# One merged order for six expert jobs: the 192-token job's weight pieces placed between the chunks of the five 64-token jobs

## The reference

```python
def moe_swiglu(h, w_router, w_gate, w_up, w_down):
    xt = h.reshape(-1, d)                       # 264 x 1024
    top_v, top_i = lax.top_k((xt @ w_router), 2)
    wts = jax.nn.softmax(top_v, axis=-1)
    comb = jnp.einsum('tk,tke->te', wts, one_hot(top_i, 8))
    for e in range(8):
        he = silu(xt @ w_gate[e]) * (xt @ w_up[e])      # 1024 -> 3584
        y = y + comb[:, e:e + 1] * (he @ w_down[e])     # 3584 -> 1024
```

## Time and profile before

| | |
|---|---|
| median of 3 runs | 1712.05 us (1707.0 to 1712.27) |
| profiled execution, its own time | 1708.26 us |
| span of its instructions | 1706.4 us |
| TensorE busy | 1490.1 us, 87% |
| VectorE, ScalarE, GpSimd busy | 771.7, 633.9, 141.8 us |
| moved by DMA | 511.54 MB, mean 300 GB/s |
| mean granted clock of TensorE | 0.954 |

### The profile page before, as it was taken

One profiled execution on the slowest core, in us unless ns is written; L12 is line 12 of the kernel. 1 busy time (PEld: TensorE's weight loads), 2 busy tenths in 40 slices (PEclk: granted clock), 3 DMA queues, 4 the chain that ended last, 5 costly groups with the idle time before them and its releaser, 6 DMA issues.

```text
span 1706.4 us, 23857 instructions
## 1 busy us (share of the span) xinstructions
PE 1490.1 (87%) x9451; PEld 1069.2 (63%) x9451; DVE 771.7 (45%) x1096; ACT 633.9 (37%) x965; POOL 141.8 (8%) x209
## 2 busy tenths in 40 slices
PE   6989889999797897999999999998777878778771
PEld 3878779988585795888888666653333433334331
DVE  2554464566466945899998555520000101001013
ACT  3632354512346555788887454520000000000002
POOL 1032100000012201850000000000000000000001
PEclk9998899999987699999999999999999999999996
DMA  9751565345553266999997656579999999999995
GB/s 359 289 229 68 204 253 196 124 161 204 203 196 141 84 244 274 420 422 402 418 391 280 234 207 237 220 263 422 421 422 421 422 422 422 422 422 422 423 422 205
DMA packets 67432, 511.54 MB, mean 300 GB/s; under 512 B 7600, under 2 KB 7871, under 8 KB 15248
## 3 DMA queue, kind: packets, MB, share of 16 engines
q1 hardware_dynamic: 63730, 496.60, 73.1%
q0 software_dynamic: 3072, 12.54, 2.0%
q10 hardware_dynamic: 542, 1.20, 0.2%
HBM read 486.44 MB, written 23.89 MB: 299 GB/s over the span
## 4 chain that ended last, share of the span: by engine, by line
PE 35%; DMA 27%; DVE 2%; issue 1%; ACT 1%; SPq 0%; POOL 0%; DVEq 0%; ACTq 0%; POOLq 0%
PE bank L2119 34%; DMA ring<-in_expert_rows_dram 26%; DMA y_rows<-arena 1%; PE bank L2647 1%; DMA fT<-y_rows,row_i 0%; DVE arena L2100 0%; PE bank L2572 0%; DVE hT L1936 0%; DVE arena L2092 0%; ACT arena L1356 0%; DVE arena L2102 0%; SPq L607 0%; POOL arena L963 0%; DVE rstd L1505 0%; ACT plain_lo L1246 0%
## 5 line engine op out<-in xcount | busy, mean ns | idle before, releaser
L2119 PE MATMUL bank<-ring,fT 128*64 128x256 f32 (+1 forms) x2928 | 415.6, 424 | 93.1 <-DMA ring<-in_expert_rows_dram 90.1
L2119 PEld LDWEIGHTS bank<-ring,fT 128*64 128x64 f32 x2928 | 198.3, 136 | 293.7 <-DMA ring<-in_expert_rows_dram 127.7
L2119 PE MATMUL bank<-parts,w_hi 128*128 128x264 f32 x1600 | 309.9, 295 | 20.2 <-DVE parts L1512 20.1
L2119 PE MATMUL bank<-w_hi,parts 128*128 128x512 f32 x1008 | 303.4, 396 | 4.3 <-issue 2.6
L548 DVE TENSOR_TENSOR w_lo<-ring,w_hi 128x1024 fp32r<-128x1024 f32 x216 | 261.4, 1227 | 61.8 <-ACT w_hi L543 48.5
L2119 PEld LDWEIGHTS bank<-parts,w_hi 128*128 128x128 f32 x1600 | 259.0, 197 | 31.2 <-issue 18.9
L543 ACT ACTIVATE w_hi<-ring 128x1024 fp32r<-128x1024 f32 x216 | 228.5, 1062 | 116.4 <-PE bank L2119 115.4
L2119 PE MATMUL bank<-parts,w_lo 128*128 128x264 f32 x800 | 232.9, 291 | 0.0
L2119 PEld LDWEIGHTS bank<-w_hi,parts 128*128 128x128 f32 x1008 | 185.3, 188 | 58.1 <-issue 19.7
L2119 PE MATMUL bank<-w_lo,parts 128*128 128x512 f32 x504 | 182.9, 390 | 0.0
L497 DVE TENSOR_TENSOR w_lo<-ring,w_hi 128x2048 fp32r<-128x2048 f32 x50 | 114.3, 2291 | 141.0 <-ACT w_hi L491 140.9
(11 more groups left out here) (465 smaller groups left out, 1359.0 us busy)
## 6 DMA issues: line engine op xcount, KB each, us to landing
ring<-in_expert_rows_dram SPq DMA_DIRECT2D x294, 1024.0 KB, 15.2
ring<-in_dense_rows_dram SPq DMA_DIRECT2D x48, 2048.0 KB, 8.2
hT<-in_expert_rows_dram SPq DMA_DIRECT2D x49, 1024.0 KB, 15.1
ring<-in_dense_rows_dram SPq DMA_DIRECT2D x8, 1408.0 KB, 5.9
x_rows<-arena SPq DMA_DIRECT2D x1, 8192.0 KB, 30.5
y_rows<-arena SPq DMA_DIRECT2D x9, 512.0 KB, 13.4
arena<-x_rows SPq DMA_DIRECT2D x8, 512.0 KB, 15.9
y_rows<-arena SPq DMA_DIRECT2D x1, 3584.0 KB, 38.6
```

Of the source, the lines that this page charges most:

```text
L2119: return pe.matmul(out, lhsT, rhs, start=start, stop=stop, skip_group_check=True)
```

## The change

The jobs 2 to 7 become one unrolled order, `MIX`. It walks through the 35 chunks of the five 64-token jobs and places the 21 pieces of the 192-token job between them, one after about two of three chunks in the first 32. A piece of the 192-token job now does its four units of 128-token products first and then the raw products of all four units; a half is given back by the latter. In the mixed order the pieces of the 192-token job are not split ahead of the previous job's end; ScalarE and VectorE split a piece's four units at its place in the order. Each 64-token chunk has gate and up in one bank (`lot_bank`), and its SiLU comes when both are complete. The x rows of the 64-token jobs are packed (`LOT_ROW`, 64 rows each), fetched once during job 0 into `x_lots`, and turned from there. Results of 64-token jobs are stored as 64 rows by two DMAs (`store_lot`). `x_rows` and `y_rows` get smaller, and so do their zero fills (12 and 5 blocks of 128 rows, in place of 16 and 7). The prefetch after the last job is now inside the branch for overflow jobs. All loops over jobs are unrolled, GpSimd's table takes three more operations, and the semaphores of the first state and the router weights are merged.

```diff
-BIG_BLOCK = JOBS + 2
+BIG_OVER = 32
+LOT_ROW = P * (BIG + 2)
+OVER_ROW = LOT_ROW + LOT * HALF_JOBS
+BIG_ROW = OVER_ROW + P * OVER
+ROW_COUNT = BIG_ROW + LOT
...
+BIG_PIECES = [(f"big_{_w}", _c) for _c in range(NCHK) for _w in ("gate", "up", "down")]
+MIX, _placed = [], 0
+for _n in range(HALF_JOBS * NCHK):
+    _k, _c = divmod(_n, NCHK)
+    MIX.append(("gate", _k, _c))
+    if _c:
+        MIX.append(("turn", _k, _c - 1))
+    if _placed and BIG_PIECES[_placed - 1][0] == "big_up" and MIX[-2 - bool(_c)][0] == "big_up":
+        MIX.append(("big_turn", None, BIG_PIECES[_placed - 1][1]))
+    MIX.append(("up", _k, _c))
+    if _c:
+        MIX.append(("down", _k, _c - 1))
+    if _c == NCHK - 1:
+        if _k + 1 < HALF_JOBS:
+            MIX.append(("x", _k + 1, 0))
+        MIX += [("turn", _k, _c), ("down", _k, _c)]
+    while _placed < min(len(BIG_PIECES), len(BIG_PIECES) * _n // BIG_OVER):
+        _w, _b = BIG_PIECES[_placed]
+        MIX.append((_w, None, _b))
+        _placed += 1
...
+        x_lots = [arena[LOT * (k % 2):LOT * (k % 2) + LOT, D * (k // 2):D * (k // 2) + D] for k in range(HALF_JOBS)]
...
-            with eng.Fori(0, FULL_JOBS - 1) as j:
-                job(j, j, "full", "full")
-            job(FULL_JOBS - 1, FULL_JOBS - 1, "full", "big")
-            job(BIG, BIG, "big", "half")
-            with eng.Fori(0, HALF_JOBS) as k:
-                half_job(k + BIG + 1)
...
+        def lot_bank(c):
+
+            return bank[2 if c % 2 == 0 else 6]
+
+        def big_slot_free(eng, n):
+
+
+            if n < AHEAD:
+                unit_free(eng, BIG - 1, NU + n - AHEAD)
+                return
+            p, q = divmod(n - AHEAD, 4)
+            if q < 3:
+                eng.wait_ge(early_units_used, 3 * (EXPERT_PIECES * BIG + p) + q + 1)
+            else:
+                name, c = BIG_PIECES[p]
+                eng.wait_ge({"big_gate": gate_full, "big_up": up_full, "big_down": down_done}[name], NCHK * BIG + c + 1)
+
+        def for_jobs(eng, job, mix, first_units):
+
+
+            for j in range(FULL_JOBS):
+                job(j, j, "mix" if j == FULL_JOBS - 1 else "full")
             eng.wait_ge(jobs_ready, 2)
             more = eng.value_load(tabi[0:1, 0:1], min_val=0, max_val=OVER)
+            mix()
             with eng.If(more > 0):
-                if first_units:
-                    first_units(EXPERTS, BIG + 1)
                 with eng.Fori(0, more) as k:
-                    job(k + EXPERTS, k + BIG + 1, "full", "full")
-            return more + EXPERTS
-
-        def turn_banks(kind):
-
-            return (0, 2) if kind == "big" else (7, 2)
+                    first_units(k + EXPERTS, k + BIG + 1)
+                    job(k + EXPERTS, k + BIG + 1, "alone")
...
+                    zeros = y_job.rearrange("q a b -> q (a b)").unsqueeze(1).broadcast_to([P, ROW_COUNT // P, D])
                     sp.dma_start(x_rows.rearrange("(j p) d -> p j d", p=P), zeros).then_inc(x_zeroed, 16)
-                    sp.dma_start(y_rows[P * (EXPERTS + 1):P * (JOBS + 3), :].rearrange("(j p) d -> p j d", p=P),
-                                 zeros[:, 0:OVER + 2, :]).then_inc(x_zeroed, 16)
+                    sp.dma_start(y_rows[OVER_ROW:BIG_ROW, :].rearrange("(j p) d -> p j d", p=P),
+                                 zeros[:, 0:OVER, :]).then_inc(x_zeroed, 16)
...
-            rest(0, 0)
-            sp.dma_start(x_raw_b, x_rows[P * BIG_BLOCK:P * BIG_BLOCK + LOT, :]).then_inc(x_raw_loaded, 16)
+            rest_with_rows(0, 0)
+            sp.dma_start(x_raw_b, x_rows[BIG_ROW:BIG_ROW + LOT, :]).then_inc(x_lots_loaded, 16)
+            for at in range(0, LOT * HALF_JOBS, P):
+                n = min(P, LOT * HALF_JOBS - at)
+                sp.dma_start(arena[0:n, D * (at // P):D * (at // P) + D], x_rows[LOT_ROW + at:LOT_ROW + at + n, :])                    .then_inc(x_lots_loaded, 16)
             sp.wait_ge(jobs_ready, 2)
             more = sp.value_load(tabi[0:1, 0:1], min_val=0, max_val=OVER)
-            first_halves(1, expert_of(1))
-            with sp.Fori(0, EXPERTS - 1) as k:
-                rest(k + 1, expert_of(k + 1))
-                first_halves(k + 2, expert_of(k + 2))
-            sp.wait_ge(y_ready, 2 * EXPERTS + 2)
-            for i in range(2):
-                sp.dma_start(y_rows[P * BIG_BLOCK:P * BIG_BLOCK + LOT, W * i:W * i + W], y_b[LOT * i:LOT * i + LOT, :])\
-                    .then_inc(y_last_stored, 16)
+            for j in range(1, FULL_JOBS):
+                e = expert_of(j)
+                first_halves(j, e)
+                rest_with_rows(j, e)
+            big_expert = expert_of(BIG)
+            lot_experts = [expert_of(BIG + 1 + k) for k in range(HALF_JOBS)]
+            y_due = {min(UNIT_AT[item] // 2 + 1 + HALVES + 3, 2 * len(STREAM) - 1): item for item in LAST_DOWN[:-1]}
+            for m in range(2 * len(STREAM)):
+                name, k, c = STREAM[m // 2]
+                sp.wait_ge(raw_used, unit_count(BIG, 2 * (m - HALVES) + 1))
+                h = 2 * kinds.index((name[4:] if k is None else name, c)) + m % 2
+                e = big_expert if k is None else lot_experts[k]
+                sp.dma_start(half_ring[m % HALVES], expert_rows[bass.ds(e * (NH * P) + P * h, P), :])\
+                    .then_inc(half_loaded[m % HALVES], 16)
+                if m == HALVES + 3:
+                    store_y(BIG)
+                if m in y_due:
+                    item = y_due[m]
+                    sp.wait_ge(y_ready, y_count(item))
+                    if item[0] == "big_down":
+                        sp.dma_start(y_rows[P * (BIG + 1):P * (BIG + 2), :], y_job.rearrange("q a b -> q (a b)"))\
+                            .then_inc(y_row_stored, 16)
+                        store_lot(BIG_ROW, y_b)
+                    else:
+                        store_lot(LOT_ROW + LOT * item[1], y_lot)
...
             with sp.If(more > 0):
                 with sp.Fori(0, more) as k:
-                    rest(k + EXPERTS, expert_of(k + EXPERTS))
-                    first_halves(k + EXPERTS + 1, expert_of(k + EXPERTS + 1))
-            njobs = more + EXPERTS
-            last = sp.snap(njobs * P)
-            end = sp.snap(loaded_count(njobs, 0))
-            sp.wait_ge(y_ready, 2 * njobs + 2)
-            sp.dma_start(y_rows[bass.ds(last, P), :], y_job.rearrange("q a b -> q (a b)")).then_inc(y_last_stored, 16)
-            for h in range(HALVES):
-                sp.wait_ge(half_loaded[h], end)
+                    e = expert_of(k + EXPERTS)
+                    at = sp.snap(k * P + OVER_ROW)
+                    first_halves(k + EXPERTS, e)
+                    sp.wait_ge(gath_full, 2 * k + 2 * (BIG + 1))
+                    sp.dma_start(x_raw, x_rows[bass.ds(at, P), :]).then_inc(x_raw_loaded, 16)
+                    rest(k + EXPERTS, e)
+                    sp.wait_ge(y_ready, 2 * k + 2 * EXPERTS + 4)
+                    sp.dma_start(y_rows[bass.ds(at, P), :], y_job.rearrange("q a b -> q (a b)")).then_inc(y_row_stored, 16)
+            sp.wait_ge(y_row_stored, 16 * more + 16 * (BIG + 2))
+            sp.wait_ge(y_ready, y_count(LAST_DOWN[-1]))
+            store_lot(LOT_ROW + LOT * LAST_DOWN[-1][1], y_lot)
...
-            pool.wait_ge(y_last_stored, 48)
+            pool.wait_ge(y_row_stored, 16 * (BIG + 2))
+            pool.wait_ge(y_lots_stored, 32 * (HALF_JOBS + 1))
...
         @block.scalar
+            def mix():
+
+                for item in MIX:
+                    name, k, c = item
+                    if name in ("big_gate", "big_up", "big_down"):
+                        for q in range(4):
+                            n, u = UNIT_AT[item] + q, big_unit(item, q)
+                            if q % 2 == 0:
+                                act.wait_ge(half_loaded[n // 2 % HALVES], loaded_count(BIG, n // 2))
+                            big_slot_free(act, u)
+                            act.activation(hi_slots[u % AHEAD], raw_unit(n), ACT.Copy).then_inc(hi_ready, 1)
+                    if name == "up":
+                        act.wait_ge(raw_used, mix_count(item, 3))
+                        act.activation(g_act_lot[:, c % 2, :], lot_bank(c)[:, 0:256], ACT.Silu).then_inc(g_ready, 1)
+                    if name == "big_gate":
+                        act.wait_ge(raw_used, mix_count(item, 3))
+                        act.activation(g_act[:, c % 2, :], bank[0][:, :], ACT.Silu)
+                        act.activation(g_act_b[:, c % 2, :], bank[1][:, 0:256], ACT.Silu).then_inc(g_ready, 1)
...
         @block.vector
+            def mix():
+
+                for item in MIX:
+                    name, k, c = item
+                    if name in ("big_gate", "big_up", "big_down"):
+                        for q in range(4):
+                            n, u = UNIT_AT[item] + q, big_unit(item, q)
+                            dve.wait_ge(hi_ready, unit_count(BIG, u))
```

(72 more changed lines are left out.)

296 lines of the change are left out of this document (133 added, 163 removed).

## The result

The changed kernel takes 1613.76 us (median of 4 runs, 1609.3 to 1615.3), against 1712.16 us (4 runs) for the kernel before: a ratio of 0.9425, 95% interval 0.9396 to 0.9454. It is faster by 98 us. In the profiled executions the span is 92.7 us shorter: the joint stage, from the first product of the six jobs to the end of the last result's copy, takes 80.4 us less, the tail behind it 14.2 less, and the stage begins 1.9 us later. The forecast was 1591 us with a range of 1570 to 1635; of the 121 us forecast, 23 did not come.

The account below looks back on a forecast made before the run. TensorE bounds the 192-token job, the weight stream the 64-token jobs and, narrowly, the joint stage. 1706.4 minus 105.4 (joint stage) minus 12.5 (tail) is 1588.5; with 1.9 outside the span 1590.4, given as 1591 us, range 1570 to 1635.

Parts of the forecast that it names:

- The bounds: Joint stage: the stream needs 614 us against TensorE's 594, so the stream ends last, by 20 us.
- TensorE's 594 us: TensorE's work in the joint stage: 387 us for the five 64-token jobs, 207 for the 192-token job.
- the one on ScalarE and VectorE: Joint stage: splits take 3.1 us under 3.5 us of cover; failing cover costs 2.3 us a piece, 48 at most.
- the 2 us for the buffers: Joint stage: buffers held at the peaks cost the stream 2 us, bounds 0 and 46.
- The clock: Expert stage: a falling clock is no rival of weight, as the granted clock is 1.00 in every window.
- The tail: Behind the last result: 6.3 us to the first gather instead of 18.8, a gain of 12.5 us.
- B: Joint stage: TensorE becomes the bound through exposed splits or costlier switches, 1604 to 1640 us in all; chance 0.20.
- A: Joint stage: the stream bounds it at its full rate, 1572 to 1604 us in all; chance 0.62.
- C: Joint stage: stream loses rate through late buffers or splits beside it, 1635 us in all, 1680 with waits; chance 0.10.
- signs of being wrong: Joint stage at 390 GB/s with SyncE waiting; TensorE waiting for `w_lo`, DMA share below 1; first gather 10 us behind.
- D: Joint stage: a piece's splits overlap with nothing, 125 us more, 1683 to 1721 us in all; chance 0.03.
- The lower stream rate: Joint stage: the skill's 358 GB/s limit, an estimated 1700 us in all; less than 0.01 of the chance 0.10.

Follow-up runs that it names:

- raw products first: Changed kernel with the raw products of all four units ahead of the 128-token products in each 192-token piece: 1592.47 us, 0.9304.
- half of the stream: Changed kernel with each half load of the joint stage bringing only half of its columns: 1570.75 us, 0.9167.
- Products in the waits: Changed kernel with twelve unread products in front of each of the 13 pieces that had waited: 1598.69 us, 0.9349.
- dummy loads: Changed kernel with seven half loads put back behind the last real one, and a wait for them at the end: 1621.39 us, 0.9486.
- the wait in front of the branch: Changed kernel with SyncE's wait for the last result in front of the conditional branch, no dummy loads: 1613.8 us, 0.9437.

## Why the prediction came out as it did

**The bounds** were right. The stream needs what was reckoned: with raw products first the joint stage is 631.5 us (930.2 to 1561.7) against 627.5, and it fills the stage at share 1.00. The start, 930.2, was 0.3 us off. TensorE's 594 us are borne out from the other side: with half of the stream the stage is 612 us, and less its 14 us of waits 598, with a clock of 0.99 over the stage.

**The step that was mis-sized** is the one on ScalarE and VectorE, and with it the 2 us for the buffers. The prediction said that the cover of the splits was thin, priced its failure at 2.3 us a piece and 48 us in all, and then dropped it: "While the stream is the bound, such waits fall into time in which TensorE would wait anyway." The waits came, 37.7 us at 13 pieces. But the stage is bound by the stream only on average. After a 192-token piece TensorE is 9 us behind the halves, by the prediction's own reckoning; with 3 us of waiting and an estimated 2 to 3 us lost to half clock on top, no buffer was free for a while, and the stream had a hole. As the stream is busy at nearly all other times, it can't make these microseconds good. The price of one wait was too low as well, 2.3 us for the 2.65 to 3.04 measured, and the waits came at places that the sum 3.1 against 3.5 us left out: behind chunk 0, which has no `down` to cover the splits, behind a result copy, and above all where the half itself had only just landed. The stage is 23 us longer than with the waits covered (654.7 against 631.5); I had 2.

**The clock** was dismissed wrongly: "no rival of weight", because the windows of before show 1.00 with waits in them and without. Those waits were at most 1.9 us long; the new ones are 2.65 to 3.04 us. Products in the waits show what the clock made of them: 16 of the 23 us. The windows of before hold no wait of that length, so the row should have been read together with the length of the waits in it. Length alone does not settle it, though: four of the 13 waits left the clock at 1.00. What decides between them is open. The Trainium skill ("TensorE: Matmul & The Clock Gate", section "HAM oscillation — how this bites in real kernels") describes the pattern, a wait for data that leaves TensorE at half clock for the products behind it. Here the waits are for a split unit, and the trace agrees at nine of 13, with a granted 0.50 behind one of 2.8 us.

**The tail** was forecast to win 12.5 us and won 14.2: the result to the first gather takes 3.9 us (1584.9 to 1588.7) instead of 18.8 (forecast 6.3), as the store landed in 2.4 us. The parts were not what the prediction had: it gave the branch 5.25 us and the landing some 6.5. With the dummy loads alone put back, 11.9 of the 14.2 us return (40.7 against 28.8), and the wait in front of the branch costs nothing that can be told.

**The rivals.** The total, 1613.8, is in B's interval, but what happened is neither A nor B: the stream was not saturated, and TensorE's work was not the bound by itself, since its 612 us alone and the stream's 631.5 with the waits covered are both well under 654.7. It is nearest to C, a stream held back by late buffers, with the price of B's waits. One of the prediction's signs of being wrong came true as well: TensorE waits for `w_lo` with the DMA share below 1 (37.7 us, share 0.97). B named the exposed splits, at up to 48 us; C named the late buffers, at 46. D, splits that overlap with nothing, did not come: the waits are for one unit and not for four. The lower stream rate that the prediction set beside C did not show either: with raw products first the stream held 412 GB/s over the whole stage, its slow start included.

**What stays open.** The remaining 4 us of the stage with raw products first: its first two windows of 5 us have DMA shares of 0.35 and 0.54, so it is the start, with all buffers full, that costs more than reckoned: those shares leave 5.5 us of the stream unused, where 1.8 were reckoned. I did not try to begin the joint order earlier, beside the full jobs; they leave little room for it, since TensorE is busy all the time there and the DMA share is 0.98 to 1.01. What lets the clock fall behind one wait and not behind another of the same length is not known. And why the joint stage ended earlier with the dummy loads is not known either.

## What to carry to other kernels

When two kinds of work with different bounds are interleaved, first add up each resource over the joint stage, then look at the smallest piece: what does the scarce engine do between a tile's landing and the tile's first product that depends on a conversion? Put work there that needs no conversion; here a change of order inside the piece was worth 23 us, a quarter of what the interleaving itself had won. And price a wait of TensorE by what follows it, half clock and buffers given back late, not by its own length alone.

## What the runs showed that was not expected

**A busy engine is cheaper than an idle one.** 156 products of no use, 13 groups of 2.7 us, made the kernel 16 us faster.

**The branch was slow because of the dummy loads.** With these inputs every engine jumps over the body of the branch. TensorE's wait at this place, from the waits around the end of three kernels: before the change,

```profile
PE bank L2743 <- issue: 5.3, 1, 5.3
```

after it,

```profile
PE bank L2878 <- issue: 2.2, 1, 2.2
```

and after it with the dummy loads put back:

```profile
PE bank L2884 <- issue: 4.7, 1, 4.7
```

ScalarE shows the same, 5.5, 2.0 and 4.6 us, and SyncE 5.25 us before the change against 0.46 with the late branch and no loads under way. With seven halves of 1 MB under way the jump takes TensorE 2.5 us longer. A likely cause is that the engine fetches its code behind the jump by DMA, beside these loads. The Trainium skill ("Runtime: NRT & Kernel Launch", section "Instruction fetch mechanics") says that a taken branch forces a DMA fetch of the target if the target lies outside the code already fetched. 4.7 against 2.2 us fits that, but no run here shows the fetch itself.
